# Value products on the whole turned probabilities and one masked copy of them

## The reference, cut to what matters

```python
kb = with_prev(k)      # keys of the previous and of the own tile of 128
vb = with_prev(v)
s = jnp.einsum('bnqhgd,bnkhd->bnhgqk', qb, kb) * (ATTN_HEAD_DIM ** -0.5)
dist = qi - kj
band = (dist >= 0) & (dist < WINDOW)
...
probs = p / (jnp.sum(p, axis=-1, keepdims=True) + jnp.exp(sink - m))
o = jnp.einsum('bnhgqk,bnkhd->bnqhgd', probs, vb)
```

## Time and profile before

| what | value |
|---|---|
| runs | 3070.65, 3071.48, 3074.03 us |
| median | 3071.48 us |
| the profiled execution | 3076.11 us |
| its span, first to last instruction | 3074.4 us |
| TensorE busy | 3015.2 us, 98% |
| VectorE busy | 1611.4 us, 52% |
| ScalarE busy | 1208.9 us, 39% |
| GpSimd busy | 113.3 us, 4% |
| mean granted TensorE clock | 0.992 |

### The profile page before, as it was taken

One profiled execution on the slowest core, in us unless ns is written; L12 is line 12 of the kernel. 1 busy time (PEld: TensorE's weight loads), 2 busy tenths in 40 slices (PEclk: granted clock), 3 DMA queues, 4 the chain that ended last, 5 costly groups with the idle time before them and its releaser, 6 DMA issues.

```text
span 3074.4 us, 40199 instructions
## 1 busy us (share of the span) xinstructions
PE 3015.2 (98%) x16040; PEld 2498.9 (81%) x16040; DVE 1611.4 (52%) x2621; ACT 1208.9 (39%) x1980; POOL 113.3 (4%) x110
## 2 busy tenths in 40 slices
PE   7999999999999999999999999999999999999999
PEld 4897878888788788888889878888887978878887
DVE  4876565433466667333365756633336575643333
ACT  3654543222265554322235545422224555432222
POOL 0011000000001100000000110000000011000000
PEclk9999999999999999999999999999999999999999
DMA  6443344222434343322243344222224333322223
GB/s 250 160 153 100 124 161 151 96 96 97 136 103 127 93 134 110 108 98 96 96 137 114 103 117 144 101 98 96 96 96 137 125 109 100 124 82 96 96 96 103
DMA packets 138585, 358.35 MB, mean 117 GB/s; under 512 B 38304, under 2 KB 38560, under 8 KB 135328
## 3 DMA queue, kind: packets, MB, share of 16 engines
q1 hardware_dynamic: 134048, 347.40, 34.0%
q10 hardware_dynamic: 4352, 8.39, 0.7%
HBM read 326.38 MB, written 29.36 MB: 116 GB/s over the span
## 4 chain that ended last, share of the span: by engine, by line
PE 83%; DVE 6%; issue 4%; ACT 3%; DVEq 1%; DMA 1%; SPq 1%; POOL 0%; POOLq 0%; ACTq 0%
PE gb L1769 63%; PE gb L1798 7%; PE gb L2121 4%; PE mb L1966 2%; DVE tmp_c L1469 1%; DVE inv_c L1472 1%; DVE w_lo L1158 1%; PE mb L1939 1%; ACT sc L941 1%; PE mb L1881 1%; PE mb L1961 1%; ACT sc L933 1%; DMA ada_buf<-in_ada_w 1%; PE mb L2032 0%; PE gb L1780 0%
## 5 line engine op out<-in xcount | busy, mean ns | idle before, releaser
L751 ACT ACTIVATE w_hi<-w_raw 128x1024 fp32r<-128x1024 f32 x492 | 518.6, 1057 | 1049.2 <-PE gb L1769 981.4
L1769 PE MATMUL gb<-h_hi,w_hi 128*128 128x512 f32 x2304 | 910.4, 395 | 18.9 <-DVE w_lo L1158 12.0
L1769 PE MATMUL gb<-h_lo,w_hi 128*128 128x512 f32 x2304 | 908.0, 394 | 0.0
L1769 PE MATMUL gb<-h_hi,w_lo 128*128 128x512 f32 x2304 | 907.6, 394 | 0.0
L1158 DVE TENSOR_TENSOR w_lo<-w_raw,w_hi 128x1024 fp32r<-128x1024 f32 x492 | 600.7, 1222 | 496.0 <-ACT w_hi L751 494.6
L1769 PEld LDWEIGHTS gb<-h_hi,w_hi 128*128 128x128 f32 x2304 | 435.9, 189 | 115.9 <-DVE w_lo L1158 15.2
L1769 PEld LDWEIGHTS gb<-h_lo,w_hi 128*128 128x128 f32 x2304 | 436.3, 189 | 94.7 <-issue 6.5
L1769 PEld LDWEIGHTS gb<-h_hi,w_lo 128*128 128x128 f32 x2304 | 435.9, 189 | 91.2
L1769 PE MATMUL gb<-hid_hi,w_hi 128*128 128x512 f32 x704 | 274.0, 389 | 0.0
L1769 PE MATMUL gb<-hid_hi,w_lo 128*128 128x512 f32 x704 | 273.9, 389 | 0.0
L1769 PE MATMUL gb<-hid_lo,w_hi 128*128 128x512 f32 x704 | 273.9, 389 | 0.0
(11 more groups left out here) (287 smaller groups left out, 3432.0 us busy)
## 6 DMA issues: line engine op xcount, KB each, us to landing
w_raw<-in_wstream SPq DMA_DIRECT2D x492, 512.0 KB, 3.3
ada_buf<-in_ada_w SPq DMA_DIRECT2D x24, 1024.0 KB, 7.6
x<-in_x SPq DMA_DIRECT2D x4, 2048.0 KB, 10.0
out<-x ACTq DMA_DIRECT2D x16, 512.0 KB, 3.0
xs<-in_x SPq DMA_DIRECT2D x12, 512.0 KB, 6.0
scratch_nt<-st_nt SPq DMA_DIRECT2D x16, 256.0 KB, 2.6
scratch_at<-st_at SPq DMA_DIRECT2D x16, 256.0 KB, 2.9
scratch_kd<-st_kd SPq DMA_DIRECT2D x16, 256.0 KB, 3.1
```

Source lines behind the costliest of these rows:

```text
L751: act.activation(w_hi[s][:, :], w_raw[s][:, :], ACT.Copy).then_inc(w_high.sem, 1)
L1769: last = pe.matmul(bank(j), w, r, start=(i == 0), stop=(i == n - 1))
```

## The change

The sum over own and older values can be written in another way. With the probabilities P in turned form, the own values V and the older values W, the kernel before forms (P under the mask) x V + (P under the opposite mask) x W. The changed kernel forms (P under the mask) x (V - W) + P x W. So one masked copy is needed and one whole copy.

- ScalarE copies each group's turned probabilities from PSUM into `pT[g][1]`, whole (`whole_probs`), after the second `normalise` of the tile, in all four tiles.
- VectorE multiplies `pT[g][1]` by `tri` into `pT[g][0]`, one product instead of two, and reads SBUF instead of PSUM. It waits for ScalarE's copy instead of TensorE's turn.
- GpSimd forms V - W of the tile into one of two new buffers `v_step` (`value_step`), once per tile, ahead of `invert_sum`.
- TensorE's value products take `v_step` and the older values; it waits for three more signals per tile.

```diff
+    v_step = [sb(f"v_step{k}", [P, KV_HEADS * HEAD_DIM]) for k in range(2)]
...
+                def value_step(t):
+
+                    if t >= 2:
+                        pool.wait_ge(attn_out.sem, attn_out.at(b, t - 1))
+                    elif b:
+                        pool.wait_ge(attn_out.sem, attn_out.at(b - 1, t + 3))
+                    if t == 0:
+                        pool.wait_ge(a_evac, emptied(b, J_Z, "A"))
+                    old = proj[:, t - 1, QKW:ATW] if t else v_prev[:, :]
+                    pool.tensor_tensor(v_step[t % 2][:, :], proj[:, t, QKW:ATW], old, ALU.subtract).then_inc(v_stepped.sem, 1)
+
                 attention_power(0)
                 for t in range(NT):
+                    value_step(t)
                     invert_sum(t, 0)
                     invert_sum(t, 1)
...
+                def whole_probs(t, g):
+
+                    act.wait_ge(probs_turned.sem, probs_turned.at(b, 2 * t + g + 1))
+                    act.activation(pT[g][1][:, :, :], m(g), ACT.Copy).then_inc(probsT_whole.sem, 1)
...
                     normalise(t, 1)
+                    whole_probs(t, 0)
+                    whole_probs(t, 1)
                     split_gate(g + 2)
                     gate_out(g + 1)
...
                     normalise(t, 1)
+                    whole_probs(t, 0)
+                    whole_probs(t, 1)
                     if c:
                         delta_out(c - 1)
                     split_gate(g + 1)
...
                 def split_probs(t, g):
 
-                    dve.wait_ge(probs_turned.sem, probs_turned.at(b, 2 * t + g + 1))
-                    dve.tensor_tensor(pT[g][0][:, :, :], m(g), each_head(tri[:, :]), ALU.mult)
-                    dve.tensor_tensor(pT[g][1][:, :, :], m(g), each_head(gtm[:, :]), ALU.mult).then_inc(probsT_ready.sem, 1)
+                    dve.wait_ge(probsT_whole.sem, probsT_whole.at(b, 2 * t + g + 1))
+                    dve.tensor_tensor(pT[g][0][:, :, :], pT[g][1][:, :, :], each_head(tri[:, :]), ALU.mult
+                                      ).then_inc(probsT_ready.sem, 1)
...
                     for g in range(2):
                         pe.wait_ge(probsT_ready.sem, probsT_ready.at(b, 2 * t + g + 1))
-                        for part, tile in enumerate((t, t - 1)):
+                        pe.wait_ge(probsT_whole.sem, probsT_whole.at(b, 2 * t + g + 1))
+                        if g == 0:
+                            pe.wait_ge(v_stepped.sem, v_stepped.at(b, t + 1))
+                        v_old = proj[:, t - 1, QKW:ATW] if t else v_prev[:, :]
+                        for part, values in enumerate((v_step[t % 2][:, :], v_old)):
                             for kv in range(KV_HEADS):
-                                v = (proj[:, tile, QKW + 64 * kv:QKW + 64 * kv + 64] if tile >= 0
-                                     else v_prev[:, 64 * kv:64 * kv + 64])
+                                v = values[:, 64 * kv:64 * kv + 64]
                                 o_ap = m(0)[64 * kv:64 * kv + 64, 2 * g:2 * g + 2, :]
                                 last = pe.matmul(o_ap, v, pT[g][part][:, kv::2, :], start=(part == 0), stop=(part == 1))
```

More of the change, by code:

```diff
@@ L450, in layer_program @@
     maxed, exped, probs_ready = [sig(s, 2 * NT) for s in ("maxed", "exped", "probs_ready")]
-    probs_turned, probsT_ready = sig("probs_turned", 2 * NT), sig("probsT_ready", 2 * NT)
+    probs_turned, probsT_ready, probsT_whole = [sig(s, 2 * NT) for s in ("probs_turned", "probsT_ready", "probsT_whole")]
+    v_stepped = sig("v_stepped", NT)
     attn_out, attn_saved = sig("attn_out", NT), sig("attn_saved", NT)
```

## The result

| | before | after |
|---|---|---|
| median, us | 3073.75 (13 runs, 3070.65 to 3077.08) | 3080.46 (13 runs, 3074.46 to 3084.14) |
| ratio | | 1.0021, interval 1.0014 to 1.0028 |

What follows compares the result with a forecast made beforehand. TensorE, busy 98% of the span, was taken as the bound. The delta-copy stall of 5.5 us less VectorE's 0.4 gave +5.1 us: 3076.6 us against the median of 3071.48, +0.17%, range 3070.5 to 3082.5.

Steps and rivals of the forecast that it cites:

- The delta copy behind two whole copies: Tile 3: ScalarE's delta copy queues behind the new copies, so TensorE's delta products start 1.36 us later; 5.5 us in four blocks.
- From there TensorE waits for nothing that stands still: After tile 3's delta products, until tile 1 of the next block, no wait takes the 1.36 us back.
- VectorE's relief in tile 0, -0.4 us: VectorE saves 1.2 us per tile, but only until tile 1's scores; 0.4 us gained in all.
- Tile 1's 0.33 us, worth nothing: Tile 1's value products lose their 0.33 us, but TensorE only waits longer for the image: no gain.
- If the image came earlier too, 1.3 us in four blocks: Tile 1: the gain if the image also arrived earlier, instead of at its own time.
- 2.2 us in each of the four blocks: Tile 2, kernel before: TensorE's stand before the first image read back from memory, read as 2.2 us per block.
- Tile 2 at nothing: Tile 2: ScalarE's copies fit its idle time of 2.48 us and VectorE idles before its splits; no cost or gain.
- TensorE's 48 waits at nothing: TensorE's added waits are for signals long there: 0; at the dearest 0.15 us each, 7 us.
- GpSimd at 0.3 us: Each 128x128 subtraction taken as 0.3 us, from the select of that width; only above 12 us would it delay the normalisation.
- list of signs that it would be wrong: Masked product above 0.75, copies done before the second group's turn, subtraction above 1 us, or clock below 1 in tile 3.
- The trace shows no such lock: A VectorE product with two SBUF inputs started inside a GpSimd power and took 0.37 us, so no mutual lock was seen.
- The clock falls in the new wait: Rival, tile 3: TensorE's clock drops in the stall, 1.9 to 3.4 us per fall; at least one more fall, chance 0.31.

Runs made afterwards that it cites:

- held_scalare: Kernel before plus two ScalarE copies of a constant per tile into spare tiles, each waiting for TensorE's turn, read by nobody: 3081.11 us, ratio 1.0021.
- delta_copy_first: Changed kernel with ScalarE's copy of the delta output put ahead of the two whole copies in tiles 2 and 3: 3077.11 us, ratio 1.0007.
- subtraction_alone: Kernel before with GpSimd's subtraction of older from own values added once per tile, its result read by nobody: 3074.08 us, ratio 1.0000.
- one_product_vectore: Kernel before with one masked product per group on VectorE instead of two, TensorE using it for both parts: 3075.06 us, ratio 1.0005.
- gap_filled_mended: Changed kernel with delta copy first, one sweep step moved from tile 1 to tile 0, ten gate products in the image wait: 3057.71 us, ratio 0.9947.
- fill_before_delta: Changed kernel with six gate products moved ahead of the delta products in tiles 2 and 3, one left behind the value products: 3078.56 us, ratio 1.0015.
- gap_filled_before: Kernel before with ten later gate products taken forward into TensorE's wait for the image of tile 2: 3065.49 us, ratio 0.9969.

## Why the prediction was right, point by point

- **The delta copy behind two whole copies: right, to the hundredth.** 1.36 us a block was worked out, 1.35 or 1.36 was waited in all four; the sum, 5.0 by the distances and 5.4 by the wait rows, against 5.5. The distances have less because in block 0 of before the turn itself was held up by 0.45 us, and after the change it isn't. held_scalare made the stall alone, delta_copy_first removed it. "From there TensorE waits for nothing that stands still" held as well: with ScalarE's part alone the whole price reached the end.
- **VectorE's relief in tile 0, -0.4 us: right on VectorE, open on TensorE.** In the changed kernel VectorE starts the masked copy of tile 1's scores 0.14 us after ScalarE's copy in all four blocks, after 1.19, 1.04, 1.19 and 1.18 us of idle time. So nearly all of the 1.2 us per block stays there, and 0, 0.11, 0.24 and 0.01 us go on, where 0, 0.11, 0.24 and 0.02 were worked out. TensorE's wait for the weight of tile 1 is 0.01, 0.12, 0.13 and 0.39 us shorter. The distances to the image shrank by 0.3 to 0.45 us in blocks 0 to 2, instead of 0, 0.11 and 0.24. In subtraction_alone, where VectorE does all its old work, they are 17.41, 18.44 and 18.10, so the image's own arrival moves them as much. The masked copies idle 6 us more, as expected of a saving that goes forward only until the scores.
- **Tile 1's 0.33 us, worth nothing: right.** The value products take 1.94 us, the image wait grew from 8.7 to 10.3 us, 0.4 a block, and one_product_vectore gave no time. "If the image came earlier too, 1.3 us in four blocks" looks too small beside the 5.8 us, by the ratios, that the last step of gap_filled_mended brings; but filling alone showed 1. The reading "2.2 us in each of the four blocks" was the mean: before waits 2.21, 2.68, 2.53 and 1.25 us for the image.
- **Tile 2 at nothing: right.** Its distance to tile 3 is 24.15 to 24.20, as before or shorter.
- **TensorE's 48 waits at nothing: right** as far as rows go. Tile 0 to tile 1 takes 0.04 us more a block.
- **GpSimd at 0.3 us: off in size, without effect.** The usual subtraction takes 0.46 us and one took 1.89, which was on the prediction's list of signs that it would be wrong; the time didn't move, so that sign was badly chosen. The row that I took as the nearest had the width and the wrong operation.
- **"The trace shows no such lock": wrong.** I judged by one power beside one VectorE product. The runs show VectorE held up by the subtraction (below). It cost TensorE nothing that shows: subtraction_alone is at 1.0000.
- **The clock falls in the new wait: a real mechanism that didn't decide.** It happened in one of 12 blocks with that stall, and in none of the 40 blocks without it at that place; the chance of at least one fall in a run's four stalls would be 1 - (11/12)^4 = 0.29 by that count, and I had 0.31; but the price of 1.9 to 3.4 was on the high side (1.7 seen), and the changed kernel's profile has none. The falls behind the image come without the change, too.
- **The sum.** 5.1 us was forecast, 6.4 (4.3 to 8.6) measured. The rest of about 1 us is inside the interval. A fall in one of 12 stalls, at 1.7 us and four stalls a run, would be 0.6 of it, by estimate. The 2 us that delta_copy_first keeps may be the same rest; no run settles it. The sum hit its range by its main term; the terms beside it are smaller than what the runs can tell.

## What to carry to other kernels

An instruction that is given to an engine with idle time is free only if nothing urgent stands behind it in that engine's order. Look for what follows, above all where the new one waits for something late; here the remedy was to move one copy ahead of two.

Relief for an engine that isn't the bound shows only after the wait that hides it is filled. Try such a change together with the wait that hides it: alone it measured as a loss of 0.2%. With the delta copy first, the wait filled and a sweep step moved, it was part of a gain of 0.5%, of which filling alone gave 0.3.

A stall can be covered by moved work, but the cover is missed where it came from: fill_before_delta gave back about 2 of 5 us, and the filled wait for the image gave back 5.9 of 8.7 at the last turn of the delta output. Look at the list of waits again after each such move.

## What the runs showed of the hardware

**GpSimd and VectorE hold each other up.** One VectorE group of the kernel before and of subtraction_alone, which differ by the 16 subtractions alone:

```profile
L1279 DVE TENSOR_TENSOR qk<-proj,a_rs 128x640 f32<-128x640 f32 x16 | 13.1, 817 | 16.9 <-POOL a_rs L690 16.9
```

```profile
L1293 DVE TENSOR_TENSOR qk<-proj,a_rs 128x640 f32<-128x640 f32 x16 | 14.7, 920 | 16.8 <-POOL a_rs L692 16.8
```

With the subtractions the product of the queries takes 0.10 us more, on the mean of 16. In the changed kernel it is 0.92 us as well, and in one_product_vectore, which has no subtraction, 0.82. Single places in the changed kernel, one of each order of arrival:

```profile
218.25 1.89 POOL L725 TENSOR_TENSOR v_step<-proj 128x128 f32<-128x128 f32 x1
...
218.24 0.37 DVE L1495 TENSOR_TENSOR inv_c<-inv_c,tmp_c 64x207 f32<-64x207 f32 x1
218.53 1.28 DVE L1484 TENSOR_TENSOR pT<-pT,tri 128x512 f32<-128x512 f32 x2
...
263.81 0.45 POOL L725 TENSOR_TENSOR v_step<-proj 128x128 f32<-128x128 f32 x1
263.95 0.99 DVE L1302 TENSOR_TENSOR qk<-proj,a_rs 128x640 f32<-128x640 f32 x1 [2.14 <-POOL a_rs L692]
```

At 218.24 VectorE is first by 0.01 us, with two inputs in SBUF, and two masked products of the same kind follow; they end at 219.81 and the subtraction at 220.14, after 1.89 us instead of 0.45. At 263.95 VectorE's product starts inside the subtraction and takes 0.99 us instead of 0.81. The Trainium skill (SBUF — State Buffer, Who interferes with whom) says that a VectorE instruction with two SBUF inputs contends with a GpSimd instruction that reads SBUF, and that the shared port pair is an exclusive lock. These rows agree with it; the 0.18 us that VectorE lost at 263.95 are part of the 0.31 that the subtraction still had to run. The power in the earlier trace rows doesn't: a VectorE product inside its 2.11 us took its usual 0.37. So a long span of GpSimd on few elements need not hold VectorE, and its rows can't be used to deny the lock for an operation on full width.

**Two gaps of 2 us are not alike for the clock.** Behind the wait for the image, 1.25 to 3.17 us long in the kernels that keep it, the granted clock fell in 30 of 32 blocks. With ten products put there, in none of 20. Behind the wait for the weight in tile 1 (1.55 to 2.12 us where the sweeps weren't moved) it fell in four of 40, three of them in the profile of gap_filled_before at 1.78, 1.93 and 2.05 us, while 2.02, 2.04 and 2.12 us elsewhere left it at 1.00. All four are in kernels where VectorE makes both masked products (four of 16 blocks); in the six kernels that give it one and keep the sweeps, the waits are 1.55 to 1.91 us and it fell in none of 24. Behind the new wait of 1.36 to 1.39 us it was one of 12. So the length of a wait didn't decide it. What TensorE does ahead of the image wait is to turn the queries (0.60 and 0.27 us) behind its last gate products; which property of it counts, no run here shows. The price is shown: with a fall the stretch from the image to the turn of tile 2 takes 16.7 to 19.6 us instead of 15.1 to 15.6 (16.25 in the block of before whose image wait was only 1.25).
